# A hybrid decoder layer on one core: float32 conditioning chunks singly between main chunks, small matmuls one per weight tile, three PSUM banks for the mixers, the output projection in two parts

## The reference, cut to what matters

```
mod = silu(c) @ ada_w + ada_b                      # c: 1 + 8 vectors; ada_w (2048, 12288)
sh1, sc1, g1, sh2, sc2, g2 = split(mod, 6)
h = rms_norm(x) * (1 + sc1) + sh1
proj = h @ w_in                                    # (2048, 18448)
y_a = 16 HGRN2 heads, state 128x128 each           # "hg"
y_b = 8 mLSTM heads, memory 128x256 each           # "ml"
merged = sigmoid(ga) * y_a + sigmoid(gb) * y_b
x = x + g1 * (merged @ w_out)                      # (2048, 2048)
h = rms_norm(x) * (1 + sc2) + sh2
a, g = split(h @ w_up)                             # (2048, 11264)
x = x + g2 * ((gelu(causal_conv(a)) * g) @ w_down) # (5632, 2048)
y = rms_norm(x, final_norm_w)
```

## Time and profile before

| | |
|---|---|
| median of 3 runs | 2760.88 us (2757.1 to 2763.0) |
| the profiled execution's own time | 2762.37 us |
| its span, first to last instruction | 2760.8 us |
| TensorE matmuls busy | 2586.7 us, 94% |
| VectorE, ScalarE, GpSimd busy | 1397.2, 1285.5, 458.1 us |
| mean granted TensorE clock | 0.932 of 2.4 GHz |
| data read | 431 MB, mean of all traffic 167 GB/s |

### The profile page before, as it was taken

How to read it: one execution, slowest core, us unless ns; L and a number is a source line. 1 busy time by engine, 2 the same in 40 slices (tenths; PEclk the granted TensorE clock), 3 DMA queues, 4 the chain that set the end, 5 groups by cost and what they waited for, 6 DMA issues and landing times.

```text
span 2760.8 us, 46789 instructions
## 1 busy us (share of the span) xinstructions
PE 2586.7 (94%) x17745; PEld 2383.9 (86%) x17745; DVE 1397.2 (51%) x1602; ACT 1285.5 (47%) x1577; POOL 458.1 (17%) x514
## 2 busy tenths in 40 slices
PE   5779999999999999999999989898999999999997
PEld 3559988888888988888888876798999999999997
DVE  4554454354344455555565456555555555544443
ACT  4654444444454545534444344335555455443332
POOL 2100032232232232212222122110000000011000
PEclk9789998898898998999999997799999999999998
DMA  7846554454454455555556556554555555565552
GB/s 228 269 127 203 175 161 132 140 154 138 132 154 140 146 167 164 177 178 170 153 185 192 171 170 204 178 161 158 166 167 160 167 159 172 163 199 162 168 168 89
DMA packets 424717, 460.08 MB, mean 167 GB/s; under 512 B 16676, under 2 KB 414412, under 8 KB 423330
## 3 DMA queue, kind: packets, MB, share of 16 engines
q1 hardware_dynamic: 410064, 409.26, 48.4%
q0 software_dynamic: 11408, 45.54, 5.3%
q10 hardware_dynamic: 3099, 3.14, 0.4%
HBM read 431.48 MB, written 26.39 MB: 166 GB/s over the span
## 4 chain that ended last, share of the span: by engine, by line
PE 79%; issue 7%; DVE 4%; DMA 4%; ACT 3%; POOL 2%; ACTq 1%; POOLq 0%; DVEq 0%; SPq 0%
PE ps L449 22%; PE ps L450 21%; PE ps L451 21%; DMA raw<-in_ada_w 2%; PE ps L463 2%; DVE wlo L1111 2%; PE R L429 1%; ACT whi L781 1%; PE R L592 1%; PE R L576 1%; PE R L653 1%; PE R L598 1%; PE R L600 1%; PE R L586 1%; PE ps L473 1%
## 5 line engine op out<-in xcount | busy, mean ns | idle before, releaser
L1111 DVE TENSOR_TENSOR wlo<-raw,whi 128x1024 fp32r<-128x1024 f32 x776 | 1036.0, 1352 | 863.4 <-ACT whi L781 848.4
L449 PE MATMUL ps<-xh,whi 128*128 128x288 f32 x3968 | 1238.7, 312 | 47.7 <-issue 29.7
L450 PE MATMUL ps<-xl,whi 128*128 128x288 f32 x3968 | 1192.4, 301 | 0.0
L451 PE MATMUL ps<-xh,wlo 128*128 128x288 f32 x3968 | 1192.1, 300 | 0.0
L781 ACT ACTIVATE whi<-raw 128x1024 fp32r<-128x1024 f32 x776 | 808.5, 1055 | 781.4 <-PE ps L451 649.2
L449 PEld LDWEIGHTS ps<-xh,whi 128*128 128x128 f32 x3968 | 769.6, 194 | 81.5 <-issue 58.7
L450 PEld LDWEIGHTS ps<-xl,whi 128*128 128x128 f32 x3968 | 767.3, 193 | 16.7 <-issue 15.1
L451 PEld LDWEIGHTS ps<-xh,wlo 128*128 128x128 f32 x3968 | 767.2, 193 | 0.0
L463 PE MATMUL ps<-whi,cs 128*18 128x256 f32 x768 | 216.6, 313 | 10.2 <-DVE wlo L1111 10.1
L463 PE MATMUL ps<-wlo,cs 128*18 128x256 f32 x768 | 212.4, 308 | 0.0
L450 PE MATMUL ps<-ffl,whi 128*128 128x288 f32 x704 | 208.4, 296 | 0.0
(11 more groups left out here) (342 smaller groups left out, 2151.6 us busy)
## 6 DMA issues: line engine op xcount, KB each, us to landing
raw<-in_w_in SPq DMA_DIRECT2D x288, 512.0 KB, 4.0
raw<-in_ada_w SPq DMA_DIRECT2D x192, 512.0 KB, 4.7
raw<-in_w_up SPq DMA_DIRECT2D x176, 512.0 KB, 3.7
raw<-in_w_down SPq DMA_DIRECT2D x88, 512.0 KB, 3.7
raw<-in_w_out SPq DMA_DIRECT2D x32, 512.0 KB, 3.8
S<-in_state_hgrn POOLq DMA_DIRECT2D x16, 512.0 KB, 5.5
out<-S POOLq DMA_DIRECT2D x16, 512.0 KB, 4.3
C<-in_state_mlstm_C POOLq DMA_DIRECT2D x8, 1024.0 KB, 8.0
```

The source lines that it names most:

```text
L449: mm(o, whi[:, s, kk, cols], hi[:, kt0 + kk, :], start=first and kk == 0, stop=False)
L450: mm(o, whi[:, s, kk, cols], lo[:, kt0 + kk, :], start=False, stop=False)
L451: x = mm(o, wlo[:, s, kk, cols], hi[:, kt0 + kk, :], start=False, stop=last and kk == KC - 1)
L1111: TT(wlo[:, s], raw[:, s], whi[:, s].bitcast(F32), ALU.subtract).then_inc(lo_done, 1)
```

## The change

Seven edits go together.

1. A conditioning chunk is no longer split. TensorE multiplies `raw` as float32 with `cs`, now 32 float32 columns (9 used, the rest zero). There is one matmul for each of the 4 row tiles, and row tile kk writes to its own 32 PSUM partitions, `acc[32*kk:32*kk+32]`. `sel` (128 rows) adds the four parts in the turn. ACT and DVE do nothing for such a chunk. SP reloads its buffer when TensorE has used it.
2. Conditioning chunks stand singly: `HG_KINDS` has `"sssa"` twelve times and `"ssss"`, `ML_KINDS` has 32 s and 12 a. Letters are chunks now. Their sums gather in a PSUM bank of their own (`ab`), beside `ps`.
3. The stage ada2 is gone. Its 32 chunks stand singly in the first 128 main chunks of w_up (`UP_KINDS`). hg stages have 12 conditioning chunks instead of 8, ml stages 12 instead of 16. The total stays 192.
4. `hg_step` and `ml_step` yield after each small matmul, all 8 weight tiles of a chunk take one, and what is left goes on in the next chunk instead of being issued in one go.
5. The heads have 3 banks of `R`, not 4. Some operations now wait for others to free a bank: the mean square of an hg head waits for its new state, an ml head broadcasts its gate rows in two pieces, and its state update is in other steps. The chunks at which steps are due are tables (`HG_DUE`, `ML_DUE`, `OUT_DUE`, and those for TensorE).
6. w_out is in two parts of its contraction. N_P1 is 24 chunks with input tiles 0 to 11 (heads 0 to 5 of ml, ready by then), while the last two ml heads are computed. N_P2 is 8 chunks with tiles 12 to 15. DVE adds the parts in `mixo`, and GpSimd instead of DVE adds the residual.
7. `dno`, `sqd`, `sqf` and the square-root row have other places in SBUF.

```diff
-HG_BLOCKS = "ssassssassss"
-ML_BLOCKS = "ssassassasas"
+HG_KINDS = "sssa" * 12 + "ssss"
+ML_KINDS = "sssa" + "sssassa" * 5 + "ssa" + "ss"
+UP_KINDS = "sssasssasssasssassss"
...
+HG_DUE = {0: 0, 1: 1, 2: 2, 3: 4, 5: 6, 6: 10, 7: 10, 8: 11, 9: 12}
+HG_DUE_PE = {2: 2, 4: 5, 6: 7, 8: 11}
+HG_TURNS = (2, 14, 26, 38)
...
-            def ada_chunk(c, k, first, last, bank, kt0, steps):
-                pe.wait_ge(lo_done, c + 1)
+            def ada_chunk(c, k, first, last, acc, kt0):
                 s = k % RING
+                pe.wait_ge(landed[s], 4 * c + 16 * (k // RING + 1))
                 for kk in range(KC):
-                    for w in (whi, wlo):
-                        x = mm(ps[0:2 * NB, bank, 0, 0:CN], cs[:, kt0 + kk, :], w[:, s, kk, :], start=first and kk == 0 and w is whi,
-                               stop=last and kk == KC - 1 and w is wlo)
+                    x = mm(acc[32 * kk:32 * kk + 32, 0:CN], cs[:, kt0 + kk, :], raw[:, s, kk, :], start=first, stop=last)
                 x.then_inc(used, 1)
...
                 if o == 6:
                     for c in range(1, NSUB):
                         mm(R[:, 2, SUB * c:SUB * (c + 1)], Sst[:, c - 1, :], qs[:, SUB * c:SUB * (c + 1)], start=False, stop=False, skip_group_check=True)
-                        if c % 3 == 0:
-                            yield
+                        yield
...
                 if o == 8:
                     pe.wait_ge(hg["sq"], n + 1)
-                    mm(R[:, 3, 0:T], ones[:, :], lf[:, :], start=True, stop=True).then_inc(hg["ms"], 1)
+                    pe.wait_ge(hg["snew"], n + 1 + FREE)
+                    mm(R[:, 0, 0:T], ones[:, :], rs[:, :], start=True, stop=True).then_inc(hg["ms"], 1)
...
-            stream(ada2_base(0), "a" * 8, A_ADA2, hook)
-            stream(out_base(0), "ss", 0, xparts=4)
-            with pe.Fori(1, 4) as i:
-                stream(out_base(i), "ss", 0)
+            stream(N_P1, "s" * 24, steps=turns(in_order(OUT_TURNS, OUT_DUE_PE), ml_step, 6, 3), length=3, xparts=4)
+            stream(N_P2, "s" * 8, length=1, kt0=12, halves=8)
...
-            stream(up_base(0), "ss", 0, xparts=8)
-            with pe.Fori(1, 22) as i:
-                stream(up_base(i), "ss", 0)
+            stream(up2_base(0), UP_KINDS, A_UP, xparts=9)
+            with pe.Fori(1, 8) as i:
+                stream(up2_base(i), UP_KINDS, A_UP + i)
+            with pe.Fori(0, 6) as i:
+                stream(up1_base(i), "s" * 8)
```

More of the change, by code:

```diff
@@ L103, in down_base @@
 def down_base(i):
-    return ahead(N_DOWN, i, 44, 2)
+    return ahead(N_DOWN, i, 44, 2, 44)
 A_HG = 16
[L109 to L126, removed]
+A_ML = A_HG + 4 * 3
+A_UP = A_ML + 4 * 3
@@ L437, in drain, with chunk @@
                     pass
-            def chunk(c, k, first, last, bank, hi, lo, kt0, steps=None):
-                pe.wait_ge(lo_done, c + 1)
+            def chunk(c, k, first, last, bank, hi, lo, kt0, steps, half=None):
+                pe.wait_ge(lo_done, c)
                 s = k % RING
                 for kk in range(KC):
+                    if half is not None and kk % 2 == 0:
+                        pe.wait_ge(xlo, half + kk // 2)
                     for m in range(2):
@@ L474, in ada_turn, with turns @@
                 x.then_inc(ada_cols, 1)
-            def stream(N, kinds, A0, hook=None, xparts=None):
-                due = nothing()
-                for b, kind in enumerate(kinds):
-                    pe.wait_ge(bank_free[b % 2], N[1] + b // 2 + FREE)
-                    for s in range(4):
-                        k = 4 * b + s
+            now = [0]
+            def turns(order, step, head, i):
+                for k, j, o in order:
+                    while now[0] < k:
+                        yield
+                    yield from step(j, o, head + j, i)
@@ new lines, in stream @@
+            def stream(N, kinds, a0=None, steps=None, length=4, kt0=0, xparts=None, halves=None):
+                steps = nothing() if steps is None else steps
+                for k, kind in enumerate(kinds):
+                    now[0] = k
+                    if kind == "s":
+                        q = before(kinds, k, "s")
+                        b, s = q // length, q % length
+                        if s == 0:
+                            pe.wait_ge(bank_free[b % 2], N[1] + b // 2 + FREE)
@@ L858, in ada1 @@
                     A(merged[:, bass.ds(4 * i, 4), :], xT[:, bass.ds(4 * i, 4), :], ACT.Square).then_inc(sq_done, 1)
[L860 to L863 removed]
+            with act.Fori(0, 4) as i:
                 ada1(i, True)
@@ L1056, in _ @@
+            stream(N_P2, "s" * 8, each=squares)
             root(2, R[:, 0, 0:T], 1.0 / D)
```

775 lines of the change are left out of this document (419 added, 356 removed).

## The result

The changed kernel takes 2822.77 us (median of 4 runs, 2818.52 to 2826.96), the kernel before 2761.94 in the same session. The ratio is 1.021 (95% interval 1.017 to 1.026): 2.1% slower, where 3.3% faster was forecast. The profiled execution took 2819.7 us, its span is 2818.0.

What follows compares the result with a forecast made beforehand. TensorE, busy 94% of the span, was taken as the bound through its queue, clock and idle time. Terms -62 + 11 + 43 - 24 - 68 + 10 = -90 us gave 2670 us, 3.3% faster than 2760.9; range 2575 to 2745.

Steps and rivals of the forecast that it cites:

- New waits: Stages with heads: three banks and tighter tables make steps wait for banks; +10 us, bounds -20 and +50.
- The prediction's last part: Signs of being wrong: L502's records don't overlap, or TensorE held many microseconds by `R` banks, `xl` or landing.
- The clock, -62: hg1 to ml3: single small matmuls win back 60% of 102.7 us lost to lower clock; bounds 0 and -103.
- A conditioning chunk at 1.2 us: On TensorE, four float32 matmuls partly overlapping take 1.2 us a chunk, against 1.085 before.
- the forecast's case: Conditioning chunk: one matmul's second pass runs beside the next one's first; 1.2 us, total 2670 us, chance 0.48.
- full overlap: Rival: the four matmuls of a conditioning chunk lie on top of one another; 0.55 us, total 2587 us, chance 0.22.
- the case without overlap: Rival: each matmul waits for the one before; 1.82 to 2.12 us a chunk, 2759 to 2816 us, chance 0.15.
- +43: up: 32 conditioning chunks from ada2 at 1.2 us each and 8 turns at 0.61 us add 43 us.
- +11: hg and ml: 96 conditioning chunks at 1.2 us instead of 1.085 us add 11 us.
- ada1, -24: ada1: without the split, transfers and buffer reuse set the pace; last turn near 132 us, 24 us saved.
- ada2 and out, -68: ada2 and out: 241.1 us becomes 173.5, as the last two ml heads run beside main chunks of w_out.
- Small matmuls cost the same singly: TensorE: small matmuls cost 0.22 us singly, no dearer or cheaper than in groups, so 0 us.

Runs made afterwards that it cites:

- due_later: Changed kernel with TensorE's step 2 of hg and steps 8 and 10 of ml heads, also in out, due one chunk later: 2730.59 us, ratio 0.989.
- loads_past: Changed kernel with SP issuing each conditioning load after the three main loads that follow it: 2797.36 us, ratio 1.013.
- loads_due: Changed kernel with the edits of both loads_past and due_later: 2711.6 us, ratio 0.983.
- best version: loads_due with conditioning chunks moved in ml1 to ml3, ml0's hg steps 4, 6 and ml1 to ml3's steps 1, 3, 4, 6 one chunk later: 2660.4 us.
- grouped_again: The best version (split_ml0_later) with small matmuls in groups of 2 to 4 again: 2719.67 us, ratio 0.980.
- split_ml0_later: The kernel also called best version: 2660.4 us, ratio 0.963 against the kernel before.
- same_columns: Changed kernel with the four matmuls of a conditioning chunk gathering in the same 32 PSUM partitions: 2946.68 us, ratio 1.066.
- grouped: Changed kernel with small matmuls in groups of 2 to 4 again in step 6 of hg and ml: 2918.17 us, ratio 1.055.
- loads_kinds_due: loads_due with conditioning chunks in the same ring buffer wherever possible in all ml stages: 2713.11 us, ratio 0.983.

## Why the prediction was wrong

The sum was -90, the result +61. Term by term:

**New waits, +10 with a bound of +50: the step that failed.** Idle time from hg1 to out rose by 93.5 us, of which 80 in hg1 to ml3. The prediction said that "VectorE and ScalarE have half their time free, and steps are two to three chunks apart". Spare time of an engine is no slack: what counts is the date at which TensorE wants a result against the date at which the others make it, and the tables had left zero chunks or one, where the hook of the kernel before left one more. The diff showed it for hg (step 1, which makes `kt_`, due at 1, and TensorE's step 2 at 2), and I read only the distance between steps. due_later shows the share: -92 us. The wait for a bank that the prediction had in mind, the mean square of an hg head for its new state (L665), is 3.4 us. I also did not ask what replaces the lost reader in SP's condition. The prediction counted the benefit in ada1 of loads that wait for TensorE alone, and not the cost in the streams, where such a load holds three others. loads_past gives 25 us for it alone, loads_due 19 beside due_later. The prediction's last part named landing only where a main chunk follows a conditioning one in its buffer.

**The clock, -62: right in mechanism, and nothing of it in the changed kernel.** L*(1-c) over hg1 to ml3 is 104 us there, no less than the prediction's 102.7 for the kernel before: hg1 to hg3 reached 0.95 to 0.96, as expected, and gave back 37 us, but ml0 to ml3 fell to 0.81 to 0.95 and lost 38. This is a second term that failed, and through the first: it was summed as if it did not depend on the waits. With most stalls gone it comes: in the best version the sum is 40 us, some 63 less, and singles alone are worth 59 us (grouped_again against split_ml0_later).

**A conditioning chunk at 1.2 us: too dear.** It is 0.765 us, between the forecast's case and full overlap (0.55). same_columns gives 2.03 for the case without overlap, inside my 1.82 to 2.12. The ratio is 2.65. The Trainium skill ("TensorE: Matmul & The Clock Gate", section "Measured speedup vs the span model") has 2.38 for three such matmuls, not for float32; with four in float32 the overlap is as real here. So up was +27.6 instead of +43: 32 chunks at 0.765 and 8 turns at 0.44 are 28.0. In hg and ml 96 chunks are 96*(0.765 - 1.085) = -31 by this price, instead of +11. The middle case, in which the second pass of one runs beside the first pass of the next alone, is not what these rows show. The prediction also took L562 for the only small kind with 32 output partitions. The transposes of the last 32 tokens are another, and they add 0.11 us, as full ones do.

**ada1, -24:** the last turn is at 139.3, not 132, and the stage with all before it ends 20.5 us earlier. As said there, the transfers set it: before most of the last chunks TensorE stands 0.3 to 1.0 us for a landing.

**ada2 and out, -68:** 223.2 us instead of 173.5. By stage: N_P1 168.3, where 102.4*24/32 + 41.6 + 3 + 4 = 125.4 follow from the prediction's terms; in due_later it is 127.1. That is the due table again. N_P2 is 54.9 instead of 25.6 + 17.5 + 5 = 48, and 57.4 in the best version. Of these 9 us, 5 lie in its eight chunks (35.7 us instead of 30.6, with short waits for VectorE's `xl` and `x1s` and a lower clock) and 4 in the end behind them (21.4 us instead of 17.5, of which TensorE waits 5.2 for `mixo`; before it was 1.4).

**Small matmuls cost the same singly: right.** Float32 with 128 rows and 4, 32 or 128 columns adds 0.22 us to the main intervals singly and, in the trace before, 0.44 in a pair, 0.67 for three and 0.89 for four. Something else was put at nothing: worked out at full clock, TensorE's work in hg1 to hg3 is 182 us a stage instead of 178, while hg0, without heads, has only 0.7 more. grouped has 182 too, so it is not the taking apart in step 6; no run shows from what it comes.

The best version, at 2660.4 us, comes close to the forecast of 2670, but it has another order of loads and another ml pattern besides its dates, and the closeness is partly luck. Its stages are 191, 192, 193 (hg), 182 (ml0), 161 to 165 (ml1 to ml3), 188 (out) and 591 (up), where 200, 200, 195, 168, 160 to 165, 173 and 606 were forecast: a cheaper conditioning chunk makes up for a longer ml0 and out. (The forecast's stages, with ada1 and down added, come to 2648 to 2663 and not to the 2672 of its sum.)

Left open: the three banks by themselves. No kernel gave the heads a fourth one. The waits for `dn` are not theirs, since later dates alone took them away (11.1 us to 0.7 in due_later). Of the 17 us idle of ml0 in the best version, `Vx` has 6.5, a landing 3.6 and the new state (a wait for a bank) 3.3; in grouped this wait for a bank is 15.7 us in all. Whether the banks stretch the heads in other ways is not shown. That ml0 got slower with the pattern of loads_kinds_due was seen (233.6, nearly all of it clock) and avoided with another pattern, not explained.

## What to carry to other kernels

When a hook becomes a table, compare for each step the date of its last input on the other engines with its own date, and leave more distance than looks needed: here zero and one chunk were too few, and `kt_` was cured by two. A stall was paid about twice here, as a wait and as lower clock behind it. When a buffer gets another last reader, ask what stands behind its load in the in-order queue that issues it. Then look at the waits of the bottleneck engine and not at those of its helpers: 96 us less of ScalarE's waiting took 2 us of TensorE's idle time and gave 25 us. Where small matmuls must lie between large ones, spread them singly: it changes no work, but kept the clock here.

## What the runs showed of the hardware

- Four float32 matmuls with 32 output columns of the array and 256 moving columns overlap when they write to different 32 partitions: 0.765 us for the four, against 2.03 us into the same ones (at full clock, between main matmuls).
- Matmuls with 32 input rows are dearer than full ones: over the main intervals, 512 float32 columns cost 1.245 us with 32 rows and 0.865 with 128, and 32 columns 0.45 to 0.53 against 0.22. The Trainium skill ("TensorEngine Tiling (Array Packing)", section "Key Properties") has a change of the tiling mode drain TensorE; these rows agree in sign, and it may also be part of the 0.765. It is not seen on every narrow form: a transpose with 32 output columns adds 0.11 us between main matmuls, as one with 128 does.
- The same mix of three main matmuls and one small one keeps full clock in the hg stages when TensorE came into it at full clock, and was seen at half clock for over 20 us (1009.6 to 1034 in ml0, granted clock 0.5) after a stall of 3.50 us. So in these rows what the clock costs hangs on whether TensorE stood still before, and not on the mix alone; grouped_again shows that the mix counts too.
- Executions of one kernel differ in time as they differ in granted clock: those of loads_due run from 2699.0 us at 0.948 to 2726.5 us at 0.937.
